# A hybrid DeltaNet and sliding-window block: the decay projection moved to the start of a token group, and its rows spread by transfers

## What is computed

```python
h = _rmsnorm(x, norm1_w)
gq, gk, gv, gz, gb, ga, aq, ak, av = split(h @ w_in)          # one input projection
qkv = silu(causal_conv(concat(gq, gk, gv), conv_w))           # width-4 depthwise conv
beta = sigmoid(gb)                                            # 4 heads
g = -exp(a_log) * softplus(ga + dt_bias)                      # 4 heads, log decay per token
o_gdn = gated_delta_rule(q, k, v, g, beta)                    # chunks of 64, cumulated g
    # inside: gc = cumsum(g); decay = exp(gc_i - gc_j) for i >= j
    # a = (beta k) k^T * decay below the diagonal; u, w = solve(I + a, ...)
    # q_dec = q * exp(gc); k_dec = k * exp(gc_last - gc); state scan over the chunks
o_attn = sliding_window_attention(rmsnorm(aq), rmsnorm(ak), av, sinks)
x = x + concat(gated_norm(o_gdn, z), o_attn) @ w_out
x = x + square(relu(rmsnorm(x) @ w1)) @ w2
```

## Time and profile before

| | us |
|---|---|
| median of 3 runs | 2410.79 (2410.4 to 2412.34) |
| the profiled execution | 2410.9 |
| its span, first to last instruction | 2409.3 |
| PE busy | 2368.6 (98%) |
| DVE busy | 1442.3 (60%) |
| ACT busy | 959.5 (40%) |
| POOL busy | 154.2 (6%) |
| granted TensorE clock, mean | 0.998 of full speed |

### The profile page before, as it was taken

The page is one execution under the profiler, slowest core; times in us unless marked ns, Lnnn a source line. Parts: engine busy times, 40 slices in busy tenths (PEclk is TensorE's granted clock), DMA queues, the critical chain, the costliest instruction groups (busy, mean ns, idle before and its releaser), DMA issues.

```text
span 2409.3 us, 36625 instructions
## 1 busy us (share of the span) xinstructions
PE 2368.6 (98%) x12654; PEld 1954.2 (81%) x12654; DVE 1442.3 (60%) x2125; ACT 959.5 (40%) x1719; POOL 154.2 (6%) x159
## 2 busy tenths in 40 slices
PE   6999999999999999999999999999999999999998
PEld 4888888888888888888888888888888888888886
DVE  6797662454679765255567966525456885642644
ACT  4476421223357532122346753212234664321222
POOL 0031000000003100000001200000000120000000
PEclk9999999999999999999999999999999999999999
DMA  4211222233321222223332122322432113222241
GB/s 152 96 62 63 96 96 96 96 130 123 106 79 63 80 96 97 96 96 135 118 106 70 63 88 88 104 96 94 141 119 95 68 54 105 88 98 97 92 152 66
DMA packets 63315, 232.63 MB, mean 97 GB/s; under 512 B 7392, under 2 KB 7520, under 8 KB 62544
## 3 DMA queue, kind: packets, MB, share of 16 engines
q1 hardware_dynamic: 55728, 201.98, 25.1%
q0 software_dynamic: 7456, 28.97, 3.5%
HBM read 222.54 MB, written 8.39 MB: 96 GB/s over the span
## 4 chain that ended last, share of the span: by engine, by line
PE 89%; DVE 7%; issue 2%; ACT 2%; DMA 0%; DVEq 0%; POOL 0%; ACTq 0%; POOLq 0%
PE ps L1421 87%; PE ps L1584 1%; PE ps L1647 1%; DVE nq L925 0%; DVE h_l L1357 0%; DVE acc L854 0%; DVE w_l L846 0%; DVE ti L1253 0%; DVE nq_l L930 0%; DVE state L1239 0%; DVE row L972 0%; DVE at L995 0%; DVE at L1011 0%; DVE qkvz L1022 0%; DVE qk L1014 0%
## 5 line engine op out<-in xcount | busy, mean ns | idle before, releaser
L1421 PE MATMUL ps<-h_h,w_h 128*128 128x512 f32 x2004 | 790.7, 395 | 11.3 <-DVE h_l L865 4.4
L1421 PE MATMUL ps<-h_l,w_h 128*128 128x512 f32 x2004 | 781.5, 390 | 0.0
L1421 PE MATMUL ps<-h_h,w_l 128*128 128x512 f32 x2004 | 781.5, 390 | 0.0
L846 DVE TENSOR_TENSOR w_l<-stage,w_h 128x1024 fp32r<-128x1024 f32 x381 | 466.4, 1224 | 256.9 <-ACT w_h L463 243.4
L463 ACT CAST w_h<-stage 128x1024 fp32r<-128x1024 f32 x381 | 398.3, 1045 | 544.2 <-PE ps L1421 543.8
L1421 PEld LDWEIGHTS ps<-h_h,w_h 128*128 128x128 f32 x2004 | 376.9, 188 | 106.7 <-DVE h_l L865 9.0
L1421 PEld LDWEIGHTS ps<-h_h,w_l 128*128 128x128 f32 x2004 | 377.0, 188 | 79.2
L1421 PEld LDWEIGHTS ps<-h_l,w_h 128*128 128x128 f32 x2004 | 377.3, 188 | 77.3 <-issue 1.9
L1421 PE MATMUL ps<-ff_h,w_h 128*128 128x512 f32 x1036 | 404.6, 391 | 0.0
L1421 PE MATMUL ps<-ff_h,w_l 128*128 128x512 f32 x1036 | 403.1, 389 | 0.0
L1421 PE MATMUL ps<-ff_l,w_h 128*128 128x512 f32 x1036 | 403.1, 389 | 0.0
(11 more groups left out here) (196 smaller groups left out, 1884.3 us busy)
## 6 DMA issues: line engine op xcount, KB each, us to landing
stage<-w SPq DMA_DIRECT2D x385, 512.0 KB, 3.3
x_next<-x POOLq DMA_DIRECT2D x20, 512.0 KB, 5.9
out<-xs POOLq DMA_DIRECT2D x32, 256.0 KB, 2.3
xs<-x POOLq DMA_DIRECT2D x8, 512.0 KB, 5.1
xs<-x POOLq DMA_DIRECT2D x4, 1024.0 KB, 5.4
bia<-bias POOLq DMA_DIRECT2D x1, 1024.0 KB, 5.0
cst<-con POOLq DMA_DIRECT2D x1, 448.0 KB, 3.9
cst<-con POOLq DMA_DIRECT2D x1, 192.0 KB, 3.3
```

The costliest lines, as they stand in the source:

```text
L846: dve.tensor_tensor(w_l[:, b, 0:k], stage[:, s, 0:k], w_h[:, b, 0:k].bitcast(F32), ALU.subtract).then_inc(w_lo.sem, 1)
L1421: return pe.matmul(o, a, b, start=start, stop=stop)
```

## The change

The decay projection becomes unit 0, and the conv units become 1 to 12. Its eight columns stand in the weight tile twice, at 0 to 7 and at 64 to 71. Once DVE has split the unit, `rows_low` overwrites columns 64 to 71 of the high part with the low part (`ba_lo`). Two passes for each slice, `w_h` with `h_h` and with `h_l`, then give both products at once, on output partitions 0 to 7 and 64 to 71: 16 passes in place of 24. ACT reads the first, DVE adds the second. All row arithmetic and the scans now stand at the head of the group, ahead of the conv loop, on 8 partitions.

`decay_rows`, `sel`, `rowr` and the bank ROW are gone. GpSimd stores the four cumulated rows (8 KB) to a buffer in DRAM and loads them back to all 128 partitions (`rowb`, 1 MB). ACT and DVE read `rowb` in place of the bank. Tile 0 now comes straight after unit 13 (av), tile 1 after unit 14 (ak), tiles 2 and 3 after the first and the second query unit; the transposes of av come after the third query unit, in the banks that the v and k transposes of tile 3 used. DVE's `scatter` moves ahead of the last gate unit's `split_lo`.

```diff
-U_BA, U_AV, U_AK, U_AQ, U_Z = 12, 13, 14, 15, 19
+U_BA, U_CONV, U_AV, U_AK, U_AQ, U_Z = 0, 1, 13, 14, 15, 19
...
+                pool.wait_ge(row_dve.sem, row_dve.after(g, row_dve.per_group))
+                pool.nop(nofuse=True)
+                pool.dma_start(row_copy, row[HEADS:2 * HEADS, :]).then_inc(row_saved.sem, 16)
+                pool.wait_ge(row_saved.sem, row_saved.after(g, 1))
+                pool.nop(nofuse=True)
+                pool.dma_start(rowb[:], row_copy.unsqueeze(0).to_broadcast([P, HEADS, TOK])).then_inc(row_spread.sem, 16)
...
+                split_hi(g, 0, 1)
+                act.wait_ge(unit_done.sem, unit_done.after(g, U_BA + 1))
+                act.activation(X, ps[R, A0, :], ACT.Identity, scale=prm[R, C_SGN:C_SGN + 1],
+                               bias=prm[R, C_DT:C_DT + 1]).then_inc(row_act.sem, 1)
+                act.wait_ge(row_dve.sem, row_dve.after(g, 2))
+                act.activation(E, E, ACT.Exp, scale=-1.0).then_inc(row_act.sem, 1)
+                split_hi(g, 0, 2)
+                act.wait_ge(row_dve.sem, row_dve.after(g, 4))
+                act.activation(L, U, ACT.Ln).then_inc(row_act.sem, 1)
+                act.wait_ge(row_act.sem, row_act.after(g, 3))
+                act.activation(U, L, ACT.Exp, scale=-1.0).then_inc(row_act.sem, 1)
 
...
-                    act.activation(eg[:, a], heads(ROW), ACT.Exp).then_inc(B["eg_r"].sem, 1)
+                    act.activation(eg[:, a], row_tile(t), ACT.Exp).then_inc(B["eg_r"].sem, 1)
...
+            def rows_low(g, n):
+
+                own(w_lo, g, n + 1)
+                cols = slice(HD, HD + 2 * HEADS)
+                dve.tensor_copy(w_h[:, 0, :, cols], w_l[:, 0, :, cols].bitcast(F32)).then_inc(ba_lo.sem, 1)
...
                 split_lo(g, 0, 1)
+                rd = [0]
+                def row_step(ins):
+                    ins.then_inc(row_dve.sem, 1)
+                    rd[0] += 1
+                    own(row_dve, g, rd[0])
+                dve.wait_ge(unit_done.sem, unit_done.after(g, U_BA + 1))
+                dve.wait_ge(row_act.sem, row_act.after(g, 1))
+                row_step(dve.scalar_tensor_tensor(out=X, in0=ps[HD:HD + 2 * HEADS, A0, :],
+                                                  scalar=prm[R, C_SGN:C_SGN + 1], in1=X, op0=ALU.mult, op1=ALU.add))
+                row_step(dve.scalar_tensor_tensor(out=E, in0=X, scalar=-1.0, in1=X, op0=ALU.mult, op1=ALU.max))
+                dve.wait_ge(row_act.sem, row_act.after(g, 2))
+                row_step(dve.tensor_scalar(U, E, 1.0, None, ALU.add))
+                row_step(dve.scalar_tensor_tensor(out=E, in0=U, scalar=-1.0, in1=E, op0=ALU.add, op1=ALU.subtract))
+                split_lo(g, 0, 2)
+                dve.wait_ge(row_act.sem, row_act.after(g, 4))
+                row_step(dve.tensor_tensor(E, E, U, ALU.mult))
+                row_step(dve.tensor_tensor(L, L, E, ALU.subtract))
+                row_step(dve.scalar_tensor_tensor(out=L, in0=X, scalar=0.0, in1=L, op0=ALU.max, op1=ALU.add))
+                row_step(dve.tensor_scalar(L, L, nalog[R], None, ALU.mult))
+                for t in range(TILES):
+                    tile = slice(t * P, t * P + P)
+                    row_step(dve.tensor_tensor_scan(row[R, tile], cst[R, K_ONE, :], rw[R, 3, tile], 0.0,
+                                                    ALU.mult, ALU.add))
+                assert rd[0] == row_dve.per_group
+                dve.nop(nofuse=True)
                 with dve.Fori(0, CONV // 4) as i:
...
-                                split_lo(g, i * 4, s + 2)
+                                split_lo(g, i * 4, s + 3)
...
-                    dve.tensor_tensor(sm[:, t, DGC].unsqueeze(2), heads(ROW)[:, :, P - 1:P],
+                    dve.tensor_tensor(sm[:, t, DGC].unsqueeze(2), row_tile(t)[:, :, P - 1:P],
                                       sm[:, t, NB].unsqueeze(2), ALU.subtract)
-                    dve.tensor_tensor(d1[:, a], heads(ROW), per_head(cst[:, K_CAUS, :]),
+                    dve.tensor_tensor(d1[:, a], row_tile(t), per_head(cst[:, K_CAUS, :]),
                                       ALU.add).then_inc(B["d2"].sem, 1)
...
+                for t in range(TILES):
+                    j = t - 2
                     decay(t)
                     diagonal(t)
                     bias_column(t)
-                    norm_square(j + 1)
-                    norm_low(j + 1)
+                    if t:
+                        norm_square(j + 1)
+                        norm_low(j + 1)
                     products(t)
                     split_lo(g, CONV, U_AQ + 2 + j - CONV)
                     token_rows(t)
-                    norm_apply(j)
+                    if j >= 0:
+                        norm_apply(j)
 
...
                 gather()
-                query(PAIRS - 1)
-                norm_apply(PAIRS - 1)
+                query(2)
+                norm_apply(2)
                 block_inverse()
+                split_lo(g, CONV, U_Z + 2 - CONV)
+                norm_apply(PAIRS)
+                scatter()
                 split_lo(g, CONV, U_Z + 3 - CONV)
-                scatter()
...
+                    if s == 15:
+                        rows_low(g + 1, 0)
...
+                pe.wait_ge(w_lo.sem, w_lo.after(g, 1))
+                pe.wait_ge(ba_lo.sem, ba_lo.after(g, 1))
+                pe.nop(nofuse=True)
+                for k in range(KT):
+                    n1_ready(k)
+                    mm(ps[:, A0, :], w_h[:, 0, k], h_h[:, k], k == 0, False)
+                    last = mm(ps[:, A0, :], w_h[:, 0, k], h_l[:, k], False, k == KT - 1)
+                last.then_inc(unit_done.sem, 1)
...
+                        if s == 1:
+                            pe.wait_ge(row_dve.sem, row_dve.after(g, 1))
+                        unit(g, i * 4, s + 1, A0 + (s + 1) % 2, hid)
...
-                def decay_rows(t):
-                    if t == 0:
-                        pe.wait_ge(row_dve.sem, row_dve.after(g, row_dve.per_group))
-                        pe.wait_ge(copied.sem, copied.after(g, 2))
-                        pe.nop(nofuse=True)
-                        for i in range(TILES):
-                            last = pe.transpose(ps[:, ROWT, 64 * i:64 * i + 64], row[0:64, i * P:(i + 1) * P],
-                                                cst[0:64, K_ID, 0:64])
-                        last.then_inc(B1["p_rowt"].sem, 1)
-                    else:
-                        wt(B["eg_r"], t - 1)
-                    tile = rowr[64:P, t * P:t * P + P]
-                    four(heads(ROW), lambda o, h: mm(o, sel[64:P, h], tile), B["p_gr"])
                 def tile_products(t):
 
...
+                pe.wait_ge(row_dve.sem, row_dve.after(g, row_dve.per_group))
+                pe.nop(nofuse=True)
+                for t in range(TILES):
+                    last = pe.transpose(ps[:, ROWT, 64 * t:64 * t + 64], row[0:64, t * P:t * P + P], cst[0:64, K_ID, 0:64])
+                last.then_inc(B1["p_rowt"].sem, 1)
                 tile_products(0)
+                pe.wait_ge(raw_ready.sem, raw_ready.after(g, 3 * CONV))
+                unit(g, CONV, U_AK - CONV, A0, hid)
+                tile_products(1)
                 for j in range(PAIRS):
-                    if j:
-                        pe.wait_ge(copied.sem, copied.after(g, j + 1))
-                    if j == 1:
-                        pe.wait_ge(B1["tok"].sem, B1["tok"].after(g, 1))
+                    pe.wait_ge(copied.sem, copied.after(g, j + 1))
                     unit(g, CONV, U_AQ + j - CONV, A0 + (U_AQ + j) % 2, hid)
                     norm_sum(j)
-                    if j < PAIRS - 1:
-                        tile_products(j + 1)
+                    if j < 2:
+                        tile_products(j + 2)
+                    if j == 2:
+                        wt(B["vb_r"], TILES - 1)
+                        wt(B["kd_r"], TILES - 1)
+                        for c in range(2):
+                            for t in range(TILES):
+                                at = t * P + HD * c
+                                last = pe.transpose(heads(PT + c)[:, t], avr[:, at:at + P], I)
+                        last.then_inc(vt_sum.sem, 1)
 
```

More of the change, by code:

```diff
@@ L143, in build @@
         kn = sb("kn", [P, HD + TOK])
[L144 to L146 removed]
+        row = sb("row", [64, TOK])
         bia = sb("bia", [P, 2, 2, 2, 2 * P])
@@ L200, in build @@
         I = cst[:, K_ID, :]
-        R64, A4 = slice(0, 64), slice(32, 36)
-        X, E, U, L = (rw[R64, i] for i in range(4))
+        R = slice(0, 2 * HEADS)
+        X, E, U, L = (rw[R, i] for i in range(4))
         def wide(v):
@@ L648, in tile @@
                     row_scales(t)
+                act.wait_ge(unit_done.sem, unit_done.after(g, U_AV + 1))
+                act.copy(avr[:, 0:HD], avr[:, TOK:]).then_inc(vt_ready.sem, 1)
+                act.wait_ge(vt_ready.sem, vt_ready.after(g, 1))
+                act.copy(avr[:, HD:], ps[:, A0 + 1, :]).then_inc(copied.sem, 1)
```

(19 more changed lines are left out.)

170 lines of the change are left out of this document (53 added, 117 removed).

## The result

The changed kernel takes 2426.99 us (median of 4 runs, 2425.56 to 2428.47), the kernel before 2410.89. The ratio is 1.0066, with a 95% interval of 1.0048 to 1.0083: it is slower by 16 us. The forecast was 2404, the range 2394 to 2414. The profiled execution took 2425.56 us with a span of 2424.0.

The account below looks back on a forecast made before the run. PE, busy for 98% of the span, was taken to bound the kernel. Heads of groups 1 to 3 cost 2.55 us, group 0's head gains 2.3, the tile stage 7.1: 6.85 saved from 2410.9, forecast 2404, range 2394 to 2414.

Parts of the forecast that it names:

- (1): Unit 0, the decay projection: 16 passes in place of 24 save PE 1.8 us per group.
- (a): Start of unit 0: PE waits for the copy for the two-pass weights, 0.4 us later in groups 1 to 3.
- (b): Ahead of unit 3: row arithmetic and scans on DVE delay its `w_l`, PE loses 2.25 us in groups 1 to 3.
- (c): Head of group 0: unit 1 starts earlier, fourth unit at 42.0 instead of 44.3, a gain of 2.3 us.
- (d): Start of the tile stage: PE waits for the last conv unit's SiLU, 0.7 us per group, bounds 0.4 and 1.4.
- (e): Transposes of av behind the third query unit: PE waits for tile 3's `kd_r`, 0.75 us per group, bounds 0 and 2.
- (f): Last gate unit: `scatter` now lies ahead of its `w_l`, costing PE 0.45 us per group, bounds 0 and 1.5.
- The clock falls at the stop: Rival, chance 0.15: the clock falls behind the stop at unit 3 in every group, 2409.8 us, no change.
- VectorE sets the pace of the tile stage: Rival, chance 0.12: (d), (e) and (f) reach their bounds, the tile stage's 1.77 us per group are gone, 2411 us.
- Slower: the stop at unit 3 is long: Rival, chance 0.10: the stop at unit 3 is 4.85 us per group, 2415 us; break-even 3.8.
- The head is hidden: Rival, chance 0.13: rows take less on 8 partitions or unit 3's stop is under 0.3 us, 2396 us.
- (2), (3) and (4): Tile stage savings per group: decay rows 2.0 us, wait for `at` 1.38, wait for unit 14's `w_l` 0.39.

Follow-up runs that it names:

- b1: The kernel before, with GpSimd's two memsets released by the last gate unit's `w_l`, so that they start with `scatter`: 2428.21 us.
- a1: The changed kernel with one pair of lines swapped, so the last gate unit's `w_l` stands ahead of `scatter` on DVE again: 2404.94 us.
- c1: The changed kernel with last `w_l` ahead of `scatter`, row arithmetic's end behind first conv units, av transposes one query unit later, `w_h` copy before last residual add: 2389.91 us.

## Why the prediction was wrong, step by step

| step | predicted | measured |
|---|---|---|
| (1) 16 passes | 1.8 in each group | 1.75 in groups 1 to 3, 0 in group 0 |
| (a) unit 0 later | 0.4 | 0.3 to 0.7 |
| (b) stop at unit 3 | 2.25, clock full | 2.34 to 2.7, clock full in this profile |
| (c) group 0, fourth unit | 42.0 | 42.94 |
| (d) wait for SiLU | 0.7 | 0.33 |
| (e) transposes of av | 0.75 | 1.1 shown, 0.6 when removed |
| tile stage without (f) | 2.2 saved | 3.2 saved |
| (f) last gate unit | 0.45, bounds 0 and 1.5 | 5.2 to 6.4 |

**The step that failed is (f).** Its start was right: the last norm step was forecast to end 53.3 us after tile 0's start and ended at 754.2 - 701.04 = 53.2. From there the prediction took `scatter` at its old length of 5.7 and the `w_l` at 1.2. They took 8.0 and 1.9 in group 1, 3.0 us more, and 8.8 and 1.9 in the others, 3.8 more. That is nearly all of the error, for PE wanted the `w_l` at 760.6 in group 1 and got it at 764.1, and behind each of these stops the clock fell, 1.6 to 2.0 us more. The prediction's own sign of being wrong came with it: PE waits by more than 2 us per group in the tile stage.

The durations came from a trace in which GpSimd's memsets lay beside other steps. The prediction moved `scatter` and priced it by its own row, but did not ask who else waits for the norm step ahead of it. GpSimd did, for its memsets. The earlier trace rows even held a step at 1.67 us for 0.69 beside GpSimd, and the text spoke of it, but only of the mask addition. There it was right to leave it out: the mask addition takes 0.68 in the trace after. It was used on the step that the change altered, not on those that it moved next to GpSimd's work.

The Trainium skill ("SBUF — State Buffer", who interferes with whom) would have said it, beyond the part that was cited: a `tensor_scalar` with both ends in SBUF can run in a mode that uses the ports it shares with GpSimd; whichever of the two starts first keeps them for its whole instruction, and the other stands still. The traces agree with that: the first pair ends 0.14 us behind the memset that it met last, in the kernel after and in b1, and 0.5 behind it in a1 and c1, where GpSimd was already at work when the pair began. The same section of the Trainium skill says that a step with two SBUF inputs contends with a GpSimd instruction that reads SBUF and not with one that only writes it. The traces agree here too: the 512-element block products took 1.10 and 1.16 us beside the memsets in the kernel before and 1.07 and 1.15 clear of them in the kernel after, and the `w_l` beside GpSimd's copy 1.9 for 1.2.

**The rivals.** *The clock falls at the stop* came true at another stop: not behind the 2.06 us ahead of unit 3, which left it at full speed in this profile, but behind the 3.6 to 4.4 us ahead of the last gate unit. *VectorE sets the pace of the tile stage* named (f) at its bound of 1.5 and ended at 2411; the bound was the fault, worked out without GpSimd. *Slower: the stop at unit 3 is long* had the right sign and the wrong place. *The head is hidden* is out.

**Slips in the sum.** (c) says that the chain of (b), started at 30.0, gives 42.0. By (b)'s own N + 12.95 it gives 42.95, and 42.94 was measured: the gain in group 0's head is 44.3 - 42.9 = 1.4, not 2.3. The rivals multiply a stop by four groups that the sum has in three. With three the clock rival gives 2408.4, and the slower rival's break-even is 4.4 us per group, not 3.8. None of this touches (f).

**What was right.** The tile stage saved 3.2 us before its last unit: from the unit behind the last conv unit to the end of the scores ahead of the last gate unit, without the decay unit, 69.0 us before and 65.8 after. (2), (3) and (4) gave 0.5 to 1.0 more than predicted, by which of the two values of (e) one takes, and no wait for `at` is left. The transfers hide: the load of `rowb` is issued at 639.94, lands in 7.7 us (median), and its first reader comes at 701.36. The 0.73 us at the entry of the conv loop is longer than the allowed waits of 0.25 and 0.1, and explains why (b) came out a little long. That the sum is sound otherwise is borne out by a1: with the one step in its old place the time is 2404.94, of which some 3 us are low clocks behind unit 3 in its profile. In part that is luck: the tile stage gave 1.0 us per group more than forecast, and group 0's head, the stop at unit 3 and the low clocks took that back and 2.7 us more, against the 2402.2 of the sum without (f).

## What to carry to other kernels

When a step is moved, list what every other engine releases on the steps around it, and lay those engines' rows beside its new place: a duration read from the trace holds for its neighbours there, not for itself alone. Do that first for steps on which the next weights or operands queue up, since there a delay of 3 us is a stop of PE, and the stops of 3.6 us and more cost 1.6 us or more on top, in clock. A collision between two engines is free while something that nobody waits for stands in it, and the cheapest cure is often to put the awaited step ahead of it.
